# Four-tile evacuations of a split fp32 product, taken tile by tile: at the end of its last chunk and amid the next chunk's weight slabs

## The chip, the cores and the metric
One core of one Trainium2 chip runs the whole program. The metric is the device time in microseconds (us) of one execution. The engines are named PE (matmuls), DVE (vector), ACT (scalar), POOL (GpSimd) and SP (which here issues transfers).

## The reference
Two transformer-like blocks run over 512 tokens of width 1024, one after the other. Cut to what matters here:

```python
# block 1
proj = rmsnorm(h) @ w_in                               # "w1"
h = h + concat(norm(att), norm(ssm)) @ w_out           # "wo1"
q = rmsnorm(h) @ w_mem_q                               # "wmq"
k, v = rmsnorm(mem) @ w_mem_k, ... @ w_mem_v           # "wmkv"
h = h + attention(q, k, v) @ w_mem_o                   # "wmo"
h = h + peer_ffn(rmsnorm(h))                           # queries: "p1q"
# block 2
qa, ka, va, qb, kb, vb, gl = split(h2 @ w_in_2)        # "qk", "va", "vb", "gl"
gates = sigmoid(gl + b_gate)
mixed = gates[0] * (oa @ w_proj_a) + gates[1] * (ob @ w_proj_b)   # "pa", "pb"
x = x + g1 * (mixed @ w_out_2)                         # "wo2"
x = x + g2 * peer_ffn(...)                             # queries: "p2q"
```

All is fp32. `peer_ffn`, which scores 16384 experts against every token, holds most of the time; the change touches none of it but the product that makes its queries.

## The kernel before
The program is a row of phases. Each phase is one block of instruction streams, one for each engine; at its end the engines meet at a barrier, the phase's semaphores are cleared, and they meet again (`clear` in `phase_tools`, line 80; the barrier's rows carry L83). Nothing of the next phase runs before that.

`product` (line 123) is one such phase and is called thirteen times. It multiplies `srcT` (features on partitions, `kt` slabs of 128) with weights that come in `chunks` of up to 512 columns. Each fp32 factor is split in a high and a low part, and three matmuls (high by high, low by high, high by low) are added up. The streams are these:

- SP loads the weight slabs, one for each of the `kt` steps of each chunk, up to eight ahead (lines 167 to 172), then transfers that were asked for.
- ACT rounds a slab to its high part `w_hi` (line 236). It first waits until PE has done the slab `SLABS` earlier (line 234), since `w_hi` and `w_lo` are rings of `SLABS` slabs, four or two.
- DVE subtracts to get `w_lo` (line 259), which lets PE begin the slab (line 192).
- PE runs 12 matmuls in a slab: four tiles `u` (four tiles of tokens, or of output features), three matmuls each. The last of the 12 raises `multiplied` (line 202). A chunk takes four PSUM banks, and chunks alternate between two sets of four.
- When a chunk is summed up, its four tiles are evacuated from PSUM by `evacuations` (line 206), by DVE or ACT as each tile's entry says. It waits until `multiplied` has counted the whole chunk (line 210) and then takes all four tiles one behind the other, in the same instruction stream as the splits of the weights. Where an evacuation has two operations, a wait on `step` stands between them. PE waits for the evacuation of chunk c-2 before chunk c (line 185).
- The evacuation of chunk c-1 stands in the stream behind the splits of all `kt` slabs of chunk c (lines 239 and 263), or, where a norm runs as a guest in the phase (`inside`), ahead of slab `SLABS` of chunk c (`taken_at`). That of the last chunk stands at the end of the stream (lines 243 and 267).

The thirteen calls:

| phase | chunks | kt | SLABS | guest | evacuation of a tile |
|---|---|---|---|---|---|
| w1 | 4 | 8 | 4 | HeadsNorm | copy, ACT and DVE in turn |
| wo1, wmo | 2 | 8 | 4 | none | DVE adds to `h` (L2333) |
| wmq | 2 | 8 | 4 | MemoryNorm | copy, in turn |
| wmkv | 4 | 8 | 4 | two HeadsNorm | copy, in turn (two tiles) |
| p1q, p2q | 4 | 8 | 4 | TurnedBack | copy, in turn |
| va, vb | 2 | 8 | 2 | none | copy, in turn |
| gl | 4 | 8 | 2 | none | ACT, Sigmoid (L2916) |
| pa | 2 | 2 | 2 | none | DVE multiplies (L2919) |
| pb | 2 | 8 | 2 | none | DVE multiplies, then adds (L2923, L2924) |
| wo2 | 2 | 8 | 2 | none | DVE multiplies by `g1`, then adds (L2939, L2940) |

In the trace, wo1 and wo2 share the tile name `wo`. In w1 and wmkv the guest's own copies of transposed tiles (`act_end`, `dve_end`) stand ahead of the last chunk's evacuation.

Of the kernel before, what the change touches and what calls it, by code (L numbers as in the profile page):

```python
# [118 lines left out]
ON_ACT, ON_DVE = 0, 1  # L119
# [3 lines left out]
def product(nc, tag, srcT, kt, tokens, chunks, SLABS=4, transfers=(), split=None, ahead=None, halves=None, inside=()):  # L123
# [11 lines left out]
    NCH = len(chunks)  # L135
# [5 lines left out]
    with ExitStack() as ctx:  # L141
        sb, ps, sem = phase_tools(nc, ctx, tag)
# [6 lines left out]
        x_hi_ready, x_ready, w_hi_ready, w_ready, multiplied = (  # L149
            sem(n) for n in ("x_hi_ready", "x_ready", "w_hi_ready", "w_ready", "multiplied"))  # L150
# [7 lines left out]
        for guest in inside:  # L158
            guest.place(tag, sb, sem, out, chunks_out)
        taken_at = SLABS if inside else kt  # L160
# [19 lines left out]
        def _(pe):  # L180
            for c, (src, on_tokens, units) in enumerate(chunks):
# [6 lines left out]
                for k in range(kt):  # L188
# [13 lines left out]
                    last.then_inc(multiplied, 1)  # L202
# [3 lines left out]
        def evacuations(eng, which, c, steps):  # L206
            src, on_tokens, units = chunks[c]
            cols = src.shape[2] if on_tokens else tokens
            if any(e == which for e, _ in units):
                eng.wait_ge(multiplied, kt * (c + 1))  # L210
            for u, (engine, evacuate) in enumerate(units):
                if engine != which:
                    continue
                parts = evacuate(out[:, c % 2 * 4 + u, 0:cols])
                for make in parts[:-1]:
                    make().then_inc(step[which], 1)
                    steps += 1
                    eng.wait_ge(step[which], steps)
                parts[-1]().then_inc(copied[which], 1)
            return steps  # L220

        @block.scalar
        def _(act):
            steps = 0
            for c, (src, _, _) in enumerate(chunks):
                cols = src.shape[2]
                for k in range(kt):
                    s = c * kt + k
                    if c >= 1 and k == taken_at:
                        steps = evacuations(act, ON_ACT, c - 1, steps)  # L230
# [8 lines left out]
                if c >= 1 and taken_at == kt:  # L239
                    steps = evacuations(act, ON_ACT, c - 1, steps)  # L240
# [5 lines left out]
        def _(dve):  # L246
            steps = 0
            for c, (src, _, _) in enumerate(chunks):
                cols = src.shape[2]
                for k in range(kt):  # L250
                    s = c * kt + k
                    if c >= 1 and k == taken_at:
                        steps = evacuations(dve, ON_DVE, c - 1, steps)
# [9 lines left out]
                if c >= 1 and taken_at == kt:  # L263
                    steps = evacuations(dve, ON_DVE, c - 1, steps)
# [872 lines left out]
class Activations:  # L1137
# [4 lines left out]
    LOADS, SLABS, KEPT = 4, 4, 4  # L1142
# [1939 lines left out]
```

## Time and profile before

| | us |
|---|---|
| median of 3 runs | 3961.65 (3960.06 to 3962.46) |
| profiled execution | 3968.42 |
| its span on the core | 3966.6 |
| PE busy | 3626.8 (91% of the span) |
| DVE busy | 2959.2 (75%) |
| ACT busy | 1701.3 (43%) |
| POOL busy | 736.3 (19%) |

The mean granted clock of PE is 0.954 of full speed. Times in a timeline are counted from the start of the span. The duration of an operation in a row includes its end phase, so that consecutive operations on DVE or ACT start somewhat closer together than their durations say. A bracket at a row's end gives the idle time of the engine before it and what ended it. A line with "x4" merges four instructions in a row. PEclk is the granted clock of PE, where 1.00 is 2.4 GHz and 0.50 is 1.2 GHz.

### The profile page before, as it was taken

How to read it: one execution, taken by the hardware profiler on the slowest of the kernel's cores; microseconds unless marked ns; L12 is line 12 of the kernel's file. 1: busy time of each engine (PE TensorE's matmuls, PEld its weight loads, DVE VectorE, ACT ScalarE, POOL GpSimd, SP SyncE). 2: the span in 40 equal slices, each digit the busy share in tenths (PEclk: the TensorE clock that was granted, in tenths of full speed). 3: DMA queues.
4: the chain of work that ended last, by engine and by line, in shares of the span. 5: the costliest groups of instructions: out<-in, count | busy, mean ns of one | idle time of the engine just before them, and what ended most of it. 6: DMA issues, size and time to landing. Idle time of an engine off the chain costs nothing. (4 is left out here: it accounts for less than half of the span.)

```text
span 3966.6 us, 53964 instructions
## 1 busy us (share of the span) xinstructions
PE 3626.8 (91%) x19146; PEld 3149.7 (79%) x19146; DVE 2959.2 (75%) x6469; ACT 1701.3 (43%) x3187; POOL 736.3 (19%) x523
## 2 busy tenths in 40 slices
PE   7876788999999999999698898869999999999998
PEld 5545576899999988888587655657999999888887
DVE  3654463599888889999676483343999888799998
ACT  3512343233566643333344463323334666533333
POOL 0000000000333344444000000000001333345442
PEclk9978898999999999999898998989999999999999
DMA  3261222355799899999422102213456999899997
GB/s 119 87 216 43 82 91 69 110 161 168 263 307 309 301 350 402 401 400 399 163 85 80 43 1 69 69 44 116 150 161 205 319 307 308 306 401 403 403 400 285
DMA packets 371787, 853.04 MB, mean 215 GB/s; under 512 B 36016, under 2 KB 185136, under 8 KB 368944
## 3 DMA queue, kind: packets, MB, share of 16 engines
q1 hardware_dynamic: 258816, 530.45, 38.4%
q0 software_dynamic: 73728, 268.47, 17.9%
q10 hardware_dynamic: 38976, 50.68, 3.8%
q8 instruction: 154, 2.52, 0.3%
q14 instruction: 113, 0.93, 0.1%
HBM read 753.91 MB, written 94.37 MB: 214 GB/s over the span
## 5 line engine op out<-in xcount | busy, mean ns | idle before, releaser
L1091 POOL DMA_INDIRECT p2f_row<-in_expert_u_rows,p2f_index x128 | 173.6, 1356 | 1412.5 <-POOLq L83 1130.8
L1091 POOL DMA_INDIRECT p1f_row<-in_peer_u_rows,p1f_index x128 | 183.7, 1435 | 1021.0 <-POOLq L83 724.0
L1706 PE MATMUL p1v_out<-p1a_u_hi,p1v_w_hi 128*128 128x512 f32 x768 | 300.4, 391 | 4.3 <-DVE p1v_w_lo L1688 4.3
L1706 PE MATMUL p2v_out<-p2a_u_hi,p2v_w_hi 128*128 128x512 f32 x768 | 300.1, 391 | 4.3 <-DVE p2v_w_lo L1688 4.3
L1706 PE MATMUL p1v_out<-p1a_u_lo,p1v_w_hi 128*128 128x512 f32 x768 | 300.2, 391 | 0.0
L1706 PE MATMUL p1v_out<-p1a_u_hi,p1v_w_lo 128*128 128x512 f32 x768 | 300.0, 391 | 0.0
L1706 PE MATMUL p2v_out<-p2a_u_lo,p2v_w_hi 128*128 128x512 f32 x768 | 300.0, 391 | 0.0
L1706 PE MATMUL p2v_out<-p2a_u_hi,p2v_w_lo 128*128 128x512 f32 x768 | 299.8, 390 | 0.0
L1666 ACT CAST p1a_u_hi<-p1a_u 128x1024 fp32r<-128x1024 f32 x128 | 135.1, 1055 | 278.7 <-PE p1v_out L1706 277.9
L1091 POOL DMA_INDIRECT p2f_row<-in_expert_v,p2f_index x128 | 194.8, 1522 | 240.4 <-DVE p2f_sum L1114 219.0
L1666 ACT CAST p2a_u_hi<-p2a_u 128x1024 fp32r<-128x1024 f32 x128 | 135.1, 1056 | 235.1 <-PE p2v_out L1706 230.3
L1091 POOL DMA_INDIRECT p1f_row<-in_peer_v,p1f_index x128 | 179.0, 1398 | 233.5 <-DVE p1f_sum L1114 210.9
L1211 PE MATMUL p1g_pre<-p_x_hi,p1a_u_hi 128*128 128x384 f32 x576 | 198.0, 344 | 3.7 <-DVE p1a_u_lo L1201 3.7
L1211 PE MATMUL p2g_pre<-p_x_hi,p2a_u_hi 128*128 128x384 f32 x576 | 197.4, 343 | 3.7 <-DVE p2a_u_lo L1201 3.7
L1211 PE MATMUL p1g_pre<-p_x_hi,p1a_u_lo 128*128 128x384 f32 x576 | 194.5, 338 | 0.0
L1211 PE MATMUL p1g_pre<-p_x_lo,p1a_u_hi 128*128 128x384 f32 x576 | 194.2, 337 | 0.0
L1211 PE MATMUL p2g_pre<-p_x_hi,p2a_u_lo 128*128 128x384 f32 x576 | 193.7, 336 | 0.0
L1211 PE MATMUL p2g_pre<-p_x_lo,p2a_u_hi 128*128 128x384 f32 x576 | 193.6, 336 | 0.0
L1685 DVE TENSOR_TENSOR p1a_u_lo<-p1a_u,p1a_u_hi 128x1024 fp32r<-128x1024 f32 x128 | 156.4, 1222 | 25.1 <-ACT p1a_u_hi L1666 24.8
L1706 PEld LDWEIGHTS p1v_out<-p1a_u_hi,p1v_w_hi 128*128 128x128 f32 x768 | 144.9, 189 | 34.6 <-DVE p1a_u_lo L1685 4.4
L1706 PEld LDWEIGHTS p2v_out<-p2a_u_hi,p2v_w_hi 128*128 128x128 f32 x768 | 144.8, 189 | 34.4 <-DVE p2a_u_lo L1685 4.4
L1114 DVE SCALAR_TENSOR_TENSOR p2f_sum<-p2f_row,p2f_weight,p2f_sum 128x1024 f32<-128x1024 f32 x127 | 162.8, 1281 | 11.4 <-DMA p2f_row<-in_expert_v,p2f_index 9.7
(702 smaller groups left out, 10825.1 us busy)
## 6 DMA issues: line engine op xcount, KB each, us to landing
p1a_u<-in_peer_u SPq DMA_DIRECT2D x128, 512.0 KB, 4.3
p1a_u<-in_peer_v SPq DMA_DIRECT2D x128, 512.0 KB, 8.4
p2a_u<-in_expert_u SPq DMA_DIRECT2D x128, 512.0 KB, 4.4
p2a_u<-in_expert_v SPq DMA_DIRECT2D x128, 512.0 KB, 9.2
gates<-p_kept SPq DMA_DIRECT2D x20, 2048.0 KB, 12.2
acts<-p1a_a ACTq DMA_DIRECT2D x128, 192.0 KB, 4.0
p1w_a<-acts SPq DMA_DIRECT2D x128, 192.0 KB, 7.2
acts<-p2a_a ACTq DMA_DIRECT2D x128, 192.0 KB, 4.1
```

The lines of the kernel that those rows point to most:

```text
L1091: self.nc.gpsimd.indirect_dma_start(self.row[:, n % self.RING, :], None, self.u_rows if dot else self.v_rows, bass.IndirectOffsetOnAxis(ap ...
L1114: V.scalar_tensor_tensor(self.sum[:], row, weight, self.sum[:], ALU.mult, ALU.add).then_inc(self.used, 1)
L1211: last = self.nc.tensor.matmul(self.pre[:, n % 2, 0:DENSE], u[:, s, k * P:(k + 1) * P], x[:, k, P:SEQ], start=(m == 0), stop=(m == 3 * DK ...
L1666: nc.scalar.copy(v_hi[:, n % VSLABS, :], v[:, n % LOADS, :]).then_inc(v_hi_ready, 1)
L1685: V.tensor_tensor(v_lo[:, n % VSLABS, :], v[:, n % LOADS, :], v_hi[:, n % VSLABS, :], ALU.subtract).then_inc(v_ready, 1)
L1706: last = nc.tensor.matmul(out[:, o, :], lhs[:, s, t * P:(t + 1) * P], rhs[:, n % VSLABS, cols], start=(n == 0 and m == 0), stop=(n == KEYS ...
```

## The change
Three things are changed in `product`, for all callers.

1. A new semaphore `tile_done`. In the very last slab of the last chunk, PE raises it after each tile's three matmuls, and `multiplied` isn't raised for that slab. The evacuation of the last chunk waits for `tile_done` tile by tile.
2. `one_each` is true where there is no guest and `kt >= SLABS + 4`: in wo1, wmo, va, vb, gl, pb and wo2. There the evacuation of chunk c-1 is taken one tile ahead of each of the slabs `SLABS` to `SLABS + 3` of chunk c.
3. Elsewhere the place of the earlier chunks' evacuations is as it was.

```diff
--- before.py
+++ after.py
@@ -146,8 +146,8 @@
         out = ps("out", [P, 8, BANK])
         loaded = [sem(f"loaded{n}") for n in range(LOADS)]
         transferred = sem("transferred")
-        x_hi_ready, x_ready, w_hi_ready, w_ready, multiplied = (
-            sem(n) for n in ("x_hi_ready", "x_ready", "w_hi_ready", "w_ready", "multiplied"))
+        x_hi_ready, x_ready, w_hi_ready, w_ready, multiplied, tile_done = (
+            sem(n) for n in ("x_hi_ready", "x_ready", "w_hi_ready", "w_ready", "multiplied", "tile_done"))
         copied = [sem("copied_by_act"), sem("copied_by_dve")]
         step = [sem("step_act"), sem("step_dve")]
 
@@ -157,6 +157,7 @@
                 eng.wait_ge(copied[which], evacuated(upto, which))
         for guest in inside:
             guest.place(tag, sb, sem, out, chunks_out)
+        one_each = not inside and kt >= SLABS + 4
         taken_at = SLABS if inside else kt
         block = ctx.enter_context(nc.Block())
 
@@ -199,18 +200,23 @@
                                 dst, lhsT, rhs = out[:, c % 2 * 4 + u, 0:tokens], ws[:, s, tile], xs[:, k, :]
                             last = nc.tensor.matmul(dst, lhsT, rhs, start=(k == 0 and n == 0),
                                                     stop=(k == kt - 1 and n == 2), skip_group_check=True)
-                    last.then_inc(multiplied, 1)
+                        if c * kt + k == NCH * kt - 1:
+                            last.then_inc(tile_done, 1)
+                    if c * kt + k < NCH * kt - 1:
+                        last.then_inc(multiplied, 1)
                     for guest in inside:
                         guest.pe(pe, c * kt + k)
 
-        def evacuations(eng, which, c, steps):
+        def evacuations(eng, which, c, steps, chosen=None):
             src, on_tokens, units = chunks[c]
             cols = src.shape[2] if on_tokens else tokens
-            if any(e == which for e, _ in units):
+            if c < NCH - 1 and any(e == which for e, _ in units):
                 eng.wait_ge(multiplied, kt * (c + 1))
             for u, (engine, evacuate) in enumerate(units):
-                if engine != which:
+                if engine != which or chosen is not None and u not in chosen:
                     continue
+                if c == NCH - 1:
+                    eng.wait_ge(tile_done, u + 1)
                 parts = evacuate(out[:, c % 2 * 4 + u, 0:cols])
                 for make in parts[:-1]:
                     make().then_inc(step[which], 1)
@@ -226,6 +232,8 @@
                 cols = src.shape[2]
                 for k in range(kt):
                     s = c * kt + k
+                    if c >= 1 and one_each and k >= SLABS:
+                        steps = evacuations(act, ON_ACT, c - 1, steps, [k - SLABS])
                     if c >= 1 and k == taken_at:
                         steps = evacuations(act, ON_ACT, c - 1, steps)
                     if c == 0:
@@ -236,7 +244,7 @@
                     nc.scalar.copy(w_hi[:, s % SLABS, 0:cols], w[:, s % LOADS, 0:cols]).then_inc(w_hi_ready, 1)
                     for guest in inside:
                         guest.act(act, s)
-                if c >= 1 and taken_at == kt:
+                if c >= 1 and taken_at == kt and not one_each:
                     steps = evacuations(act, ON_ACT, c - 1, steps)
             for guest in inside:
                 guest.act_end(act, NCH * kt)
@@ -249,6 +257,8 @@
                 cols = src.shape[2]
                 for k in range(kt):
                     s = c * kt + k
+                    if c >= 1 and one_each and k >= SLABS:
+                        steps = evacuations(dve, ON_DVE, c - 1, steps, [k - SLABS])
                     if c >= 1 and k == taken_at:
                         steps = evacuations(dve, ON_DVE, c - 1, steps)
                     if c == 0:
@@ -260,7 +270,7 @@
                                             w_hi[:, s % SLABS, 0:cols], ALU.subtract).then_inc(w_ready, 1)
                     for guest in inside:
                         guest.dve(dve, s)
-                if c >= 1 and taken_at == kt:
+                if c >= 1 and taken_at == kt and not one_each:
                     steps = evacuations(dve, ON_DVE, c - 1, steps)
             for guest in inside:
                 guest.dve_end(dve, NCH * kt)
```

## Rows read from the trace of the kernel before

**Rows 1.** The page, part 1: busy us (share) xinstructions of each engine.
```profile
PE 3626.8 (91%) x19146; PEld 3149.7 (79%) x19146; DVE 2959.2 (75%) x6469; ACT 1701.3 (43%) x3187; POOL 736.3 (19%) x523
```

**Rows 2.** Timeline, end of wo1: start us, us, engine line op [idle <-releaser].
```profile
403.93 0.39 PE L200 MATMUL wo_out<-wo_w_lo,wo_x_hi 128*128 128x512 f32 x1
...
405.97 0.39 PE L200 MATMUL wo_out<-wo_w_lo,wo_x_hi 128*128 128x512 f32 x1
406.40 2.48 DVE L2333 TENSOR_TENSOR main_h<-main_h,wo_out 128x512 f32<-128x512 f32 x4 [7.14 <-PE wo_out L200]
409.85 1.06 ACT L977 ACTIVATE n_xn<-main_h 128x1024 f32<-128x1024 f32 x1 [13.70 <-PEq L83]
```

**Rows 3.** Timeline at the end of wmq, ACT and DVE.
```profile
481.91 1.29 DVE L278 COPY mb_q<-wmq_out 128x512 f32<-128x512 f32 x2 [9.53 <-PE wmq_out L200]
...
484.06 0.40 ACT L232 CAST wmkv_x_hi<-mb_memT 128x256 fp32r<-128x256 f32 x1 [1.08 <-PEq L83]
```

**Rows 4.** Timeline of ACT in gl, around its first evacuation.
```profile
2468.50 0.62 ACT L236 CAST gl_w_hi<-gl_w 128x512 fp32r<-128x512 f32 x1 [2.10 <-PE gl_out L200]
2469.14 1.28 ACT L2916 ACT_TABLE_LOAD   x1
2470.44 2.42 ACT L2916 ACTIVATE b_mixT<-gl_out,cols 128x512 f32<-128x512 f32 x4
2472.74 0.63 ACT L236 CAST gl_w_hi<-gl_w 128x512 fp32r<-128x512 f32 x1
...
2477.28 0.62 ACT L236 CAST gl_w_hi<-gl_w 128x512 fp32r<-128x512 f32 x1 [2.71 <-PE gl_out L200]
```

**Rows 5.** Timeline of ACT at the end of gl and the start of pa.
```profile
2518.08 2.42 ACT L2916 ACTIVATE b_qkT<-gl_out,cols 128x512 f32<-128x512 f32 x4 [2.50 <-PE gl_out L200]
2521.45 0.62 ACT L232 CAST pa_x_hi<-b_oaT 128x512 fp32r<-128x512 f32 x1 [0.95 <-PEq L83]
```

**Rows 6.** Timeline of DVE in pa, both chunks' evacuations.
```profile
2534.00 2.47 DVE L2919 TENSOR_TENSOR b_mixT<-b_mixT,pa_out 128x512 f32<-128x512 f32 x4
2538.18 2.48 DVE L2919 TENSOR_TENSOR b_mixT<-b_mixT,pa_out 128x512 f32<-128x512 f32 x4 [1.70 <-PE pa_out L200]
```

**Rows 7.** Timeline of PE and DVE at the end of pb.
```profile
2588.14 0.69 DVE L259 TENSOR_TENSOR pb_w_lo<-pb_w,pb_w_hi 128x512 fp32r<-128x512 f32 x1 [2.03 <-ACT pb_w_hi L236]
...
2588.75 0.68 DVE L2923 TENSOR_TENSOR b_qkT<-b_qkT,pb_out 128x512 f32<-128x512 f32 x1
...
2589.46 0.69 DVE L2924 TENSOR_TENSOR b_mixT<-b_mixT,b_qkT 128x512 f32<-128x512 f32 x1
...
2590.07 0.68 DVE L2923 TENSOR_TENSOR b_qkT<-b_qkT,pb_out 128x512 f32<-128x512 f32 x1
...
2592.50 0.39 PE L200 MATMUL pb_out<-pb_x_hi,pb_w_lo 128*128 128x512 f32 x1
...
2598.73 0.69 DVE L2924 TENSOR_TENSOR b_mixT<-b_mixT,b_qkT 128x512 f32<-128x512 f32 x1
```

**Rows 8.** Timeline of DVE at the end of wo2.
```profile
2657.17 0.69 DVE L2940 TENSOR_TENSOR main_h<-main_h,wo_out 128x512 f32<-128x512 f32 x1
```

**Rows 9.** Timeline of DVE at the end of w1.
```profile
129.71 1.28 DVE L286 COPY b_u<-w_out 128x512 f32<-128x512 f32 x2
```

**Rows 10.** Transfers of 2160:2200, in va: issues, KB each, us to landing.
```profile
b2v_masks<-in_masks SPq DMA_DIRECT2D x1, 1536.0 KB, 8.0
```

**Rows 11.** Windows after two starts of PE: PE busy (xcount), PEclk, DMA share, GB/s.
```profile
488.70:492.70 4.00, 3.95 (x9) 0.50 0.98 345
2525.60:2529.60 4.00, 3.92 (x12) 0.64 0.12 41
```

**Rows 12.** Timeline of PE, first matmul after an idle stretch, in p1g and p1v.
```profile
1011.79 0.44 PE L1211 MATMUL p1g_pre<-p_x_hi,p1a_u_hi 128*128 128x384 f32 x1 [3.65 <-DVE p1a_u_lo L1201]
...
1409.55 0.77 PE L1706 MATMUL p1v_out<-p1a_u_hi,p1v_w_hi 128*128 128x512 f32 x1 [4.29 <-DVE p1v_w_lo L1688]
```

**Rows 13.** Waits of PE in 2510:2540, before pa: us in total, times, longest.
```profile
PE pa_out L200 <- DVE pa_w_lo L259: 7.6, 1, 7.6
```

## The prediction

> **What bounds the kernel now.** I read the page first: PE is busy 91% of the span [rows 1], nearly all of it in the expert phases, which the change doesn't touch. So the question is not which engine bounds the whole, but what ends each of the thirteen `product` phases, since each is closed off by a barrier. For that I read the timeline at the end of each. The reader is to see there that PE's last matmul isn't the end: a row of evacuations follows it, the barrier begins when the last of them is done, and nothing else is late. In wo1 the last matmul ends at 405.97 + 0.39 = 406.36, the four additions run from 406.40 for 2.48 us, to 408.88, and the next phase's first operation starts at 409.85, 0.97 later [rows 2]. In gl the last sigmoid ends at 2518.08 + 2.42 = 2520.50 and the next phase starts 0.95 later [rows 5]; in wmq it is 483.20 and 0.86 [rows 3]. The distance from the last evacuation to the next phase is nearly constant, so what shortens the evacuation shortens the program, one to one. I then read the timelines inside the phases, for the places that the moved evacuations leave and enter.
>
> **What the signal of each tile gives.** The last slab's tiles don't finish together. In wo1 the third matmul of the first tile starts at 403.93 and that of the fourth at 405.97 [rows 2]: 2.04 us for three tiles, 0.68 each. Four additions take 2.48 us of which the last is 0.68, so they start 0.60 apart. An evacuation that follows tile by tile therefore keeps up with PE, and only the fourth is left behind the last matmul.
>
> - wo1: the fourth addition starts at 406.40 as before and ends at 407.08 instead of 408.88: 1.80. wmo ends in the same pattern. Together 3.60.
> - wmq, p1q, p2q, va, vb: each engine has two copies, and DVE's pair, 1.29 us, is the later [rows 3]; the same pair stands at the other four ends. The fourth tile's copy alone takes 0.69, so 0.60 each, 3.00 together. va's 1536 KB of masks land 8.0 us after their issue [rows 10], which the trace has at 2171, some 25 us before va's end; they don't take the end's place.
> - gl: four sigmoids 2.42, one 0.69 (the second to fourth start 0.58 apart, so ACT keeps up too): 1.73 [rows 5].
> - pa: the first chunk's additions start at 2534.00, so DVE is free for another at 2536.40. Tile 4 is there at 2538.14 by [rows 6], the others 0.68, 1.36 and 2.04 earlier. The four then start at 2536.40, 2537.00, 2537.60 and 2538.20, and end at 2538.88 instead of 2538.18 + 2.48 = 2540.66. That is 1.78 at best; I take 1.70.
> - w1 and wmkv: nothing. The phase's own two copies on DVE start at 129.71 with no wait of their own before them [rows 9]: they queue behind the guest's last copy, when all tiles are long done. wmkv has the same order.
>
> **What taking one tile for each slab gives.** In pb a tile costs DVE two operations, 1.32 us from one tile to the next (2588.75 to 2590.07). The first chunk's four therefore keep DVE until 2588.75 + 4 x 1.32 = 2594.03, over a us beyond the last matmul's end, 2592.50 + 0.39 = 2592.89. The end is 2598.73 + 0.69 = 2599.42 [rows 7]. After the change the first chunk's are out of the way; the last chunk's start when its first tile is done, 2592.93 - 2.04 = 2590.89, and DVE is then the slower: three tiles of 1.32 and a last one of 0.71 + 0.69 (start to start of the pair, and the second's duration) give 2596.25. The gain is 3.17. wo2 has the same pattern at 1.33 a tile and ends at 2657.17 + 0.69 = 2657.86 [rows 8], with its last matmul as far ahead. I take 3.15 each, 6.30 together.
>
> In gl, ACT's first evacuation includes a table load of 1.28 and comes in one piece of 0.64 + 1.30 + 2.42 us ahead of the next slab's cast. Slabs are 2.10 + 0.62 = 2.72 apart. From the cast at 2468.50 to the one at 2477.28, three slabs later, it is 8.78 instead of 8.16 [rows 4]: 0.62 is lost, at the third chunk's start. One tile at a time, load and sigmoid end 0.64 + 1.30 + 0.69 = 2.63 after the cast, within the 2.72. The loss goes: 0.62. In wo1, wmo, va and vb the earlier chunk's evacuation is hidden under PE's slabs before and after, and moving it gives nothing.
>
> **What it costs.** The moved evacuations stand ahead of a weight split in DVE's or ACT's stream, in front of work that PE needs; that is what they could cost. In pb the split of a slab starts 2.72 after the one before and DVE is free 0.61 later (2588.14, 2588.75); a tile's pair takes 1.41, to 2590.16, and the next split would be due at 2590.86 [rows 7]. So 0.70 is spare on DVE, and PE has about 1.2 more, since it begins a slab that long after its `w_lo` is there. For the single operations, 0.60 to 0.69, the spare time is larger. On ACT the new place adds no wait: the cast behind it waits for a later count of `multiplied` than the evacuation does. Nothing is queued behind the waits on `tile_done` but the evacuations themselves, since all splits are over. No transfer is moved on SP's queue and nothing on POOL's. The added semaphore lengthens the clearing at most: between the last evacuation and the next phase lie 0.97 us in wo1, with 18 semaphores [rows 2], and 0.86 in wmq, with 27 by the code [rows 3]. So it isn't the count that sets it; I take zero, with 0.01 each, 0.13 in all, as the bound above.
>
> **PE's clock.** Each phase starts after an idle stretch with the granted clock at 0.50, 1.2 GHz. In wmkv it stays there over the whole 4 us, in pa it averages 0.64 [rows 11]: 9 matmuls against 12 in 4 us. A slow matmul starts 0.43 after the last, a fast one 0.23; 12 in 4.0 us are 6 slow ones (6 x 0.43 + 6 x 0.23), and that is the fewest at any product's start behind wo1 but va's. The most is 14, counted by their durations, and wmkv has 12. The phases' starts shift by a few us, so this is drawn anew. Going the full way at one start is 8 x 0.2 = 1.6 us; over a dozen starts with both signs I allow 3 either way. The Trainium skill, page "TensorE: Matmul & The Clock Gate", Part 1, says the same kernel shows different counts of cold matmuls according to when its first one falls; by that rule too the sum stays and only its spread grows. No start should change its kind: an idle of 3.65 us left the clock up (0.44 for 384 columns) and one of 4.29 let it fall (0.77) [rows 12], while the idle before pa, now 7.6 [rows 13], is shortened by no more than gl's 1.73, to 5.9, and is the shortest of those that lose more than 0.60.
>
> **The sum.** 3.60 + 3.00 + 1.73 + 1.70 + 6.30 + 0.62 = 16.95 us. On the profiled execution, 3968.42 becomes 3951.5. It stands 6.8 above the median, and I take the same gain off the median: 3961.65 - 16.95 = 3944.7.
>
> **The rivals.**
> - The ends are set by something that the timelines don't show, or the per-tile signal comes late because PE raises it only when its queue drains. Then the tails stay and only gl's 0.62 is gained: 3961.0. Against it: the 0.9 us or so behind the last evacuation in three phases with different last engines, and casts of weights, which wait on the same kind of signal amid PE's matmuls and start every 2.72 us. Chance 0.05.
> - PE's clock falls out badly: wmo (7 slow matmuls now), pa (6) and the 12s all go to 14. That is 0.2 x (7 + 8 + 6 x 2) = 5.4 us: 3950.1. Nothing speaks for it but the spread in [rows 11]. Chance 0.06.
> - ACT reloads its table at each change between sigmoid and cast, now that they alternate in gl. A slab would cost ACT 0.52 + 0.58 + 2 x 1.28 = 3.66, 0.94 over the 2.72, in 12 slabs 11.3 us: 3956.0, which is within 0.2%. Against it: the casts behind the four sigmoids have no load before them [rows 4]. The Trainium skill, page "ScalarE: Activation LUTs", section "Rules for kernel authors", says to group calls by table set and finish one before switching, which speaks against this edit; it prices a switch at 2.66 us, by which it would be 0.52 + 0.58 + 5.32 - 2.72 = 3.70 a slab and the time an estimated 3989. The same page has copies in every set, and there the trace agrees. Chance 0.03.
> - Slower: the evacuations, now in front of the weight splits, come to stand on PE's path. With rings of two slabs, whatever delays a split beyond its slack delays PE. If each were fully exposed it would cost 8 x 0.60 in wo1 and wmo, 8 x 0.60 in va and vb, 12 x 0.58 in gl and 8 x 1.32 in pb and wo2: 27.1 us, so 3971.8. It decides where a tile's operations pass 1.41 + 0.70 + 1.2 = 3.3 us for each slab in pb; they are at less than half of that [rows 7]. Chance 0.03.
>
> **How the numbers follow.** The forecast, 3944.7, has 0.83; its own range is 3941 to 3949 by the clock's 3 us either way and about 1 for the run to run spread of the median. For 8 in 10 it would do nearly alone; with the clock's rival taken in it is 3940.5 to 3950.5. A measurement can tell about 0.2%, 7.9 us, from no change: faster means below 3953.7. Faster gets 0.83 + 0.06 = 0.89 (less 0.01 for what I have not thought of: 0.88), within 0.2% gets 0.05 + 0.03 and that 0.01, 0.09, and slower 0.03.
>
> **What would show it.** In the profile after, wo1's additions stand apart, 0.68 from start to start, the last ending 0.7 after PE; pb's and wo2's last eight start some 2 us before PE's last matmul ends; gl has its sigmoids singly between casts, one table load, casts every 2.72 us throughout; pb's `w_lo` still start 2.72 apart. If the gaps of PE inside gl, pb or wo2 grow, the slower rival is at work. If the phases' ends move up and the total doesn't, the time went to the starts: PEclk in the first 4 us of each phase shows it.

## The result and the profile after

The changed kernel takes 3939.67 us (median of 5 runs, 3932.46 to 3945.17) against 3962.46 for the kernel before beside it (3960.06 to 3964.1): a ratio of 0.9944, 95% interval 0.9929 to 0.9958. The profiled execution took 3938.45, its span is 3936.6, the mean granted clock 0.957. The forecast was 3944.7 in a range of 3940.5 to 3950.5, so the direction and most of the size were right, and the time lies 0.8 us below the range. Timed on three further occasions, on three chips, it came to 3946.23, 3938.90 and 3939.61; one of the four times lies in the range. Over all 21 of its executions the mean is 3940.4 (standard deviation 5.3), over 96 of the kernel before 3962.9 (3.9). The gain is thus 22.5 us, and the standard error from these two spreads is 1.2, so some 20 to 25. The sum of the prediction was 16.95. Some 5 us are to be explained beyond it. One execution of all those reported below, of tile_only, took 4992.31 us at a granted clock of 0.692; it counts in no ratio, and without it that kernel's median is 3947.71 instead of 3947.96.

The page of the changed kernel, part 1, which answers to [rows 1]:

```profile
PE 3615.3 (92%) x19146; PEld 3144.1 (80%) x19146; DVE 2961.4 (75%) x6469; ACT 1699.8 (43%) x3187; POOL 745.2 (19%) x523
```

The same instructions run, and DVE and ACT are busy for the same time. PE is busy for 11.5 us less, with the same 19146 matmuls. A shorter tail can't do that: it takes idle time away. It is a first sign that matmuls ran at another clock, though from one pair of profiles.

The ends of the phases look as forecast. The timeline of the changed kernel at the end of wo1 (start us, us, engine, line, op, [idle before it <- releaser]), which answers to [rows 2]:

```profile
398.81 2.72 DVE L2343 TENSOR_TENSOR main_h<-main_h,wo_out 128x512 f32<-128x512 f32 x4 [7.49 <-PE wo_out L201]
...
400.42 0.39 PE L201 MATMUL wo_out<-wo_w_lo,wo_x_hi 128*128 128x512 f32 x1
402.50 1.06 ACT L987 ACTIVATE n_xn<-main_h 128x1024 f32<-128x1024 f32 x1 [11.91 <-PEq L83]
```

The four additions now begin 2.00 us ahead of PE's last end (400.81) and are through 0.72 behind it; the barrier still takes 0.97. The four additions last 2.72 instead of 2.48 us, because they follow PE's tiles, 0.68 apart. ACT in gl, around the first evacuation, answers to [rows 4], and its end to [rows 5]:

```profile
2432.73 0.62 ACT L244 CAST gl_w_hi<-gl_w 128x512 fp32r<-128x512 f32 x1 [2.10 <-PE gl_out L201]
2433.37 1.28 ACT L2926 ACT_TABLE_LOAD   x1
2434.67 0.69 ACT L2926 ACTIVATE b_mixT<-gl_out,cols 128x512 f32<-128x512 f32 x1
2435.45 0.62 ACT L244 CAST gl_w_hi<-gl_w 128x512 fp32r<-128x512 f32 x1
2435.98 0.68 ACT L2926 ACTIVATE b_mixT<-gl_out,cols 128x512 f32<-128x512 f32 x1
2438.17 0.62 ACT L244 CAST gl_w_hi<-gl_w 128x512 fp32r<-128x512 f32 x1 [1.51 <-PE gl_out L201]
...
2495.97 2.73 ACT L2926 ACTIVATE b_qkT<-gl_out,cols 128x512 f32<-128x512 f32 x4 [2.73 <-PE gl_out L201]
2499.66 0.62 ACT L240 CAST pa_x_hi<-b_oaT 128x512 fp32r<-128x512 f32 x1 [0.96 <-PEq L83]
```

The casts stay 2.72 apart (2432.73, 2435.45, 2438.17), also over the table load, which is the only one in gl; sigmoids stand singly between them. DVE in pb, one slab of the last chunk and then the end, answers to [rows 7]:

```profile
2549.08 0.69 DVE L269 TENSOR_TENSOR pb_w_lo<-pb_w,pb_w_hi 128x512 fp32r<-128x512 f32 x1 [2.03 <-ACT pb_w_hi L244]
2549.69 0.68 DVE L2933 TENSOR_TENSOR b_qkT<-b_qkT,pb_out 128x512 f32<-128x512 f32 x1
2550.40 0.69 DVE L2934 TENSOR_TENSOR b_mixT<-b_mixT,b_qkT 128x512 f32<-128x512 f32 x1
2551.80 0.69 DVE L269 TENSOR_TENSOR pb_w_lo<-pb_w,pb_w_hi 128x512 fp32r<-128x512 f32 x1 [0.70 <-ACT pb_w_hi L244]
...
2568.14 0.69 DVE L2933 TENSOR_TENSOR b_qkT<-b_qkT,pb_out 128x512 f32<-128x512 f32 x1 [1.98 <-PE pb_out L201]
...
2572.84 0.69 DVE L2934 TENSOR_TENSOR b_mixT<-b_mixT,b_qkT 128x512 f32<-128x512 f32 x1
```

The splits are 2.72 apart, with the 0.70 us of DVE's spare time that the prediction worked out in the bracket of the last of them. PE's last matmul of pb ends at 2570.15; DVE is through at 2573.53.

**All thirteen tails.** The tail is here the time from the end of a product's last matmul to the end of the barrier behind it; the next phase's first operation starts some 0.07 us later. In us, before and after: wo1 3.41, 1.62; wmo 3.40, 1.63; wmq 2.12, 1.53; p1q 2.22, 1.63; p2q 2.22, 1.64; va 2.21, 1.63; vb 2.21, 1.63; gl 3.34, 1.61; pa 3.40, 1.62; pb 7.42, 4.28; wo2 7.92, 4.75; w1 2.77, 2.78; wmkv 1.97, 1.97. The differences sum up to 16.3; with the 0.62 inside gl it is 16.9, against the 16.95 that was forecast. So the 5 us lie outside the products' ends.

### The profile page after: what moved, and what is told of

Its sections match the earlier page's. It is cut to its first block and busy times, and to the rows that moved or that the text cites. A ratio compares the mean times of both kernels' runs of the same rounds, so it can differ in the third digit from the quotient of the medians.

```text
span 3936.6 us, 53976 instructions
## 1 busy us (share of the span) xinstructions
PE 3615.3 (92%) x19146; PEld 3144.1 (80%) x19146; DVE 2961.4 (75%) x6469; ACT 1699.8 (43%) x3187; POOL 745.2 (19%) x523
## 5 line engine op out<-in xcount | busy, mean ns | idle before, releaser
L1101 POOL DMA_INDIRECT p2f_row<-in_expert_u_rows,p2f_index x128 | 189.3, 1479 | 1401.7 <-POOLq L83 1115.5
L1101 POOL DMA_INDIRECT p2f_row<-in_expert_v,p2f_index x128 | 182.6, 1427 | 233.8 <-DVE p2f_sum L1124 209.6
L1695 DVE TENSOR_TENSOR p2a_u_lo<-p2a_u,p2a_u_hi 128x1024 fp32r<-128x1024 f32 x128 | 156.5, 1222 | 23.4 <-ACT p2a_u_hi L1676 18.9
```

What stands on the lines that cost most here:

```text
L1101: self.nc.gpsimd.indirect_dma_start(self.row[:, n % self.RING, :], None, self.u_rows if dot else self.v_rows, bass.IndirectOffsetOnAxis(ap ...
L1695: V.tensor_tensor(v_lo[:, n % VSLABS, :], v[:, n % LOADS, :], v_hi[:, n % VSLABS, :], ALU.subtract).then_inc(v_ready, 1)
```

## The experiments

Each kernel ran in a comparison of five rounds with the kernel before on the same chip. The ratio and its 95% interval are of that comparison, and a gain in us is worked out from the ratio. The expectations call their rivals theory A and theory B anew in each run. First, what scatters by itself.

**before_again**: the kernel before, unchanged.

> The kernel before, once more, as a control. Theory A (the change is worth the 16.95 us of the sum, and the rest of the measured 22 us is the part of each PE start that runs at the low clock, which is drawn anew in every execution): between two profiled executions of this same kernel, single phases differ by 1 to 8 us where PE is slow for longer, and the whole by 2 to 8 us; the ratio to itself is 1.000 within 0.1%. Theory B (the change is worth 22 us, the missing 5 being a saving in some phase that I overlooked): the phases agree within 1 us between the two executions, and so does the whole within about 2 us.

3962.51 us, ratio 1.0 (0.9991 to 1.0009), span 3969.7. This set the scale for what follows: a median of such a run can be told from another to about 0.1%, 4 us. One pair of profiles can't: ahead of wo1, in code that is the same in all kernels, the modulation phase alone took 108.8 and 109.1 us in the two profiles of the kernel before, and 101.5, 109.3 and 106.0 in profiles of the changed one. So phases are compared one by one, over many profiles, and only a difference that comes back in each is read.

**after_again**, **after_third** and **after_fourth**: the changed kernel, unchanged.

> The changed kernel, once more. Theory A: the timed gain is 17 us with a scatter of some us from one set of executions to the next, so anything from 14 to 22 here; the tails behind the last matmul of the twelve affected products are as short as in the first profile to 0.1 us, while the phases that gained outside of them (the modulation phase, dif, the tile norm, p1c, p1g) come out otherwise than in the first profile. Theory B: 22 to 23 us again, with the same phases shorter as in the first profile.

3946.23 us, 0.9957 (0.9944 to 0.9970). The tails are the same as in the first profile, and the modulation phase fell back from 101.5 to 109.3 us, as theory A had it; but p1c, among the phases that theory A expected to come out otherwise, took 259.7 us again.

> The changed kernel a third time, for its mean and its phases. Theory A (locked): wmq 56.8, mat 35.6, wmo 52.0, p1q 95.9 and p1c 259.7 us once more, each within 0.3; these phases with the two norms give some 3 us over the tails' sum, and the gain is about 19 us, 16 to 22 in one set. Theory B (drawn anew): single ones of them fall back to the length of before (less the tail), and the gain is 17 on the mean.

3938.90 us, 0.9936 (0.9919 to 0.9952). The five phases that theory A names took 56.8, 35.6, 51.9, 95.8 and 259.7 us, each as it said.

> The changed kernel a fourth time, beside the run with the turned order and for the mean of its gain. Theory A (locked): 3 us over the tails' 17, so 20 on the mean of all sets, 16 to 24 in this one; wmq 56.8, mat 35.6, p1q 95.9 and p1c 259.7 us in its profile. Theory B: 17 on the mean and other lengths.

3939.61 us, 0.9943 (0.9930 to 0.9956), with 56.7, 35.6, 95.8 and 259.7 us for the four phases. Three of the four ratios of the changed kernel lie under the one that 16.95 us would give, 0.9957, and the fourth is at it.

**tile_only**: the signals of each tile alone.

> Only the signal of each tile in the last chunk; the earlier chunks are evacuated where they were. From the rows of before: wo1 and wmo 3.60, wmq, p1q, p2q, va and vb 3.00, gl 1.73, pa 1.78, together 10.1 us. In pb and wo2 nothing, since DVE is still at the first chunk's eight operations until 2594.03 when the last tile is done (2592.9), and can begin no earlier than before. Theory A: 10 us on the mean, 7 to 14 in one set. Theory B: the missed 5 us come with the shorter tails, so about 14.

```diff
-        one_each = not inside and kt >= SLABS + 4
+        one_each = False
```

3947.96 us, 0.9965 (0.9952 to 0.9978): 14 us gained, between 9 and 19, where the tails give 3.6 + 3.0 + 1.73 + 1.78 = 10.1. The end of pb on DVE:

```profile
2573.35 0.39 PE L201 MATMUL pb_out<-pb_x_hi,pb_w_lo 128*128 128x512 f32 x1
...
2579.57 0.69 DVE L2934 TENSOR_TENSOR b_mixT<-b_mixT,b_qkT 128x512 f32<-128x512 f32 x1
```

6.52 us from PE's end to DVE's, the same as 2592.89 to 2599.42 in [rows 7]: the signals alone give pb nothing, for DVE still has the first chunk in front of it.

**each_only**: the other half alone; the last chunk waits for `multiplied` as before.

> Only the earlier chunks taken one tile for each slab; the last chunk waits for the whole as before. From the rows of before: pb starts its last evacuation at 2592.93 instead of 2594.04 (1.11), wo2 as much (1.15), gl loses no 0.62 at its third chunk: together 2.9 us. The two halves give 13.0 alone and 16.95 together, as pb and wo2 gain their 2.0 each from the early tiles only when the first chunk is out of the way. Theory A: 3 us, 0 to 6 in one set. Theory B: 8 us if the missed gain lies within the products' slabs, 3 if it lies at the tails.

```diff
-                        if c * kt + k == NCH * kt - 1:
-                            last.then_inc(tile_done, 1)
-                    if c * kt + k < NCH * kt - 1:
-                        last.then_inc(multiplied, 1)
+                    last.then_inc(multiplied, 1)
...
-            if c < NCH - 1 and any(e == which for e, _ in units):
+            if any(e == which for e, _ in units):
...
-                if c == NCH - 1:
-                    eng.wait_ge(tile_done, u + 1)
```

3959.20 us, 0.9993 (0.9984 to 1.0001). Its tails are 6.32 in pb and 6.79 in wo2, 1.10 and 1.13 shorter, and gl loses its stall: 2.85 by the sum, 2.8 measured, between 0 and 6. The two halves of the change give 1.1 and 0 in pb, and 3.14 together, since each removes what the other would leave last. The times show no 5 us with this half, and some 4 beyond the tails in tile_only, within wide intervals.

**wo1_tail**: of the whole change, only wo1's last chunk follows tile by tile.

> Only wo1's last chunk is evacuated tile by tile: everything behind wo1 starts 1.80 us earlier. In the profiles so far, phases between wmq and p1c have the same length in all three executions with the old starts and another, equally constant one in all three with the changed starts. Theory A (locked): the clock's rises and falls lie on a grid of their own, phases fall on it in a fixed way behind the modulation phase, and the shift moves them on it. Then, as in the changed kernel: the norm behind wo1 0.8 us longer, wmq 1.2 shorter and mat 1.0 shorter at an unchanged wmq tail, so that more than the 1.80 is gained by the end of mat: 3.2. Theory B (drawn anew): the phases behind wo1 differ from before at random, some up, some down, and do not repeat those of the run with the delay; on the mean 1.8 us.

```diff
-        one_each = not inside and kt >= SLABS + 4
+        one_each = False
+        by_tile = tag == "wo1"
...
-                        if c * kt + k == NCH * kt - 1:
+                        if by_tile and c * kt + k == NCH * kt - 1:
...
-                    if c * kt + k < NCH * kt - 1:
+                    if not by_tile or c * kt + k < NCH * kt - 1:
...
-                if c == NCH - 1:
+                if by_tile and c == NCH - 1:
```

3958.51 us, 0.9990 (0.9981 to 0.9998): 4.0 us, between 0.8 and 7.5, from a tail that is 1.79 shorter.

**wo1_delay**: the kernel before, with 1.6 us of dead work on DVE behind wo1's last evacuation.

> The kernel before with dead work at the end of wo1: two additions of 512 columns and one of 352 on scratch, 1.6 us. Nothing else. [...] Theory A (locked): the phases from the norm behind wo1 to p1c have the lengths of the run with wo1's tail alone, each within 0.2 us; with the norm 0.8 longer, wmq 1.2 and mat 1.0 shorter the delay is nearly given back by the end of mat (+0.2), and the whole is at most about 1 us slower than before, or faster. Theory B (drawn anew): 1.6 us slower on the mean, with phases unlike those of the other run.

```diff
+            if tag == "wo1":
+                for n, cols in enumerate((BANK, BANK, DEAD)):
+                    nc.vector.tensor_tensor(w[:, n, 0:cols], w[:, 3 + n, 0:cols], w[:, 3 + n, 0:cols], ALU.add)
```

3961.18 us, 0.9991 (0.9982 to 1.0000). The delay is there, wo1's tail is 5.04 instead of 3.41, and the program is not slower for it. Three windows of each of three profiles tell what happened behind wo1: the norm, wmq, and the memory attention `mat`, in this order (us, busy time of each engine with the count of its instructions, then PEclk, DMA share and GB/s). before_again:

```profile
409.85:425.50 15.65, 5.82 (x32) 5.58 (x32) 6.57 (x13) 7.22 (x13) 0.00 (x0) 0.59 0.00 0
425.50:484.10 58.60, 48.51 (x208) 39.69 (x208) 21.91 (x39) 19.49 (x37) 0.00 (x0) 0.91 0.26 90
545.00:581.50 36.50, 34.06 (x224) 30.29 (x224) 21.01 (x72) 16.16 (x49) 0.00 (x0) 0.95 0.01 1
```

wo1_tail:

```profile
402.50:418.80 16.30, 6.52 (x32) 6.28 (x32) 6.57 (x13) 7.22 (x13) 0.00 (x0) 0.58 0.00 0
418.90:476.20 57.30, 47.21 (x208) 38.82 (x208) 21.83 (x39) 19.39 (x37) 0.00 (x0) 0.91 0.27 92
537.00:572.50 35.50, 32.58 (x224) 29.24 (x224) 21.02 (x72) 16.17 (x49) 0.00 (x0) 1.00 0.01 1
```

wo1_delay:

```profile
407.10:423.40 16.30, 6.53 (x32) 6.29 (x32) 6.57 (x13) 7.22 (x13) 0.00 (x0) 0.57 0.00 0
423.50:480.70 57.20, 47.24 (x208) 38.81 (x208) 21.82 (x39) 19.38 (x37) 0.00 (x0) 0.91 0.27 93
541.60:577.10 35.50, 32.58 (x224) 29.24 (x224) 21.02 (x72) 16.17 (x49) 0.00 (x0) 1.00 0.01 1
```

In all three the counts are 32, 208 and 224 matmuls. Only PE's busy time differs: 5.82 against 6.5 in the norm, 48.5 against 47.2 in wmq, and 34.1 against 32.6 in `mat`, where PEclk is 0.95 or 1.00. The two edited kernels, one with a tail of 1.62, the other of 5.04, agree with each other to 0.03 us and differ from the kernel before alike. From barrier to barrier the three phases changed by +0.75, -1.3 and -1.0, so nearly all of the 1.63 us of the delay came back.

**wo1_delay2**: 3.43 us of dead work, by three more operations.

> As the run with dead work at wo1's end, but 3.4 us of it instead of 1.6 (five additions of 512 columns and one of 352). Theory A (locked): the phases have the old lengths again, the norm behind wo1 15.7, wmq 58.6, mat 36.6, p1q 97.6 and p1c 261.3 us, and the delay is paid in full: 3.4 us slower than before, and some 5 slower than with the shorter delay, which gave about 1.9 us back by the end of wmo. Theory B (drawn anew at each start): these phases differ from both at random.

```diff
-                for n, cols in enumerate((BANK, BANK, DEAD)):
+                for n, cols in enumerate((BANK, BANK, BANK, BANK, BANK, DEAD)):
```

3962.35 us, 1.0004 (0.9995 to 1.0012): 1.6 us lost, between -2 and 4.8. Norm, wmq and `mat` took 15.5, 58.5 and 36.7 us from first operation to first operation, the lengths of the kernel before (15.6, 58.6 and 36.6), as theory A said. So there are sets of lengths, and a delay changes from one to the other and back. Which set comes isn't fixed by wo1's tail alone, as the next kernels show.

**pool_add**: the changed kernel, with the second operation of pb's and wo2's evacuation on POOL, each behind DVE's first.

> The changed kernel with the second operation of a tile in pb and wo2 (the addition, on SBUF alone) moved to POOL, which is idle there; DVE keeps the multiplication. Behind PE's last matmul stand now 3.4 us in pb and 3.8 in wo2 before the barrier, since DVE needs 1.32 a tile. With one operation DVE keeps pace with PE (0.68 a tile), and 0.7 on DVE and one addition on POOL are left. A row for such an addition doesn't exist in the trace; between 0.7 (as on DVE) and 2.0 us. At 1.0 the two tails shorten by about 1.6 and 2.0 us, 3.6 together; at 2.0 POOL doesn't keep pace and little is left. Both theories say the same for the tails, and for the whole 3.6 with a scatter of some us by the clock.

```diff
+        if pooled:
+            @block.gpsimd
+            def _(pool):
+                for n, add in enumerate(pooled):
+                    pool.wait_ge(copied[ON_DVE], n + 1)
+                    add(pool).then_inc(added, 1)
...
-            lambda: nc.vector.tensor_tensor(mixT[:, f, :], mixT[:, f, :], sig[:, f, :], ALU.add)]
+    def add(f):
+        return lambda pool: pool.tensor_tensor(mixT[:, f, :], mixT[:, f, :], sig[:, f, :], ALU.add)
```

In wo2 the product by `g1` goes to a buffer in SBUF instead of back into PSUM, and in both products DVE takes a tile's place again only when POOL is done with it. 3938.76 us, 0.9940 (0.9927 to 0.9953), as the changed kernel. The end of pb, DVE and POOL:

```profile
2572.53 2.73 DVE L2942 TENSOR_TENSOR b_qkT<-b_qkT,pb_out 128x512 f32<-128x512 f32 x4 [1.98 <-PE pb_out L202]
...
2573.30 4.96 POOL L2945 TENSOR_TENSOR b_mixT<-b_mixT,b_qkT 128x512 f32<-128x512 f32 x4 [9.01 <-DVE b_qkT L2942]
```

Four additions take POOL 4.96 us, 1.28 each by their mean, against 0.69 on DVE. POOL then is the slower of the two, and at this price nothing is left of the 1.6 and 2.0 us that an addition of 1.0 us would have given. It is through 3.72 us behind PE's last end (2574.54), where DVE alone is through after 3.38 (2570.15 to 2573.53); pb's tail is 4.96 instead of 4.28. Half of the 0.68 more is thus between POOL's end and the barrier's: the next phase starts 1.31 us behind the last evacuation instead of 0.97. wo2's tail is 4.66 and 4.75, the same to 0.1. The Trainium skill, page "GPSIMD Engine Reference", section "Elementwise — side-by-side cycle accounting", gives an addition of two fp32 inputs of 2048 elements as 1.96 times as long there as on DVE; here, at 512, it is 1.86 times.

**last_two**: the changed kernel, with PE's order in the last two slabs of pb and wo2 turned round, so that tiles finish further apart.

> The changed kernel, with PE's order in the last two slabs of pb and wo2 turned: tiles 1 and 2 of the last slab but one, then the same two of the last, then tiles 3 and 4 in both. Tiles 1 to 4 are then done 3.40, 2.72, 1.36 and 0 us before the last matmul's end instead of 2.04, 1.36, 0.68 and 0. DVE, at 1.32 a tile, starts 3.4 ahead and the fourth tile 0.6 behind the end, so the tails shrink from 4.28 to 2.9 in pb and from 4.75 to 3.4 in wo2: 2.7 us together if PE doesn't wait for the last slab's split, which is there about 1.4 us after the slab before begins, as the first two tiles take 1.36. Both theories say the same for the tails; for the whole 2.7 less than the changed kernel, with the clock's scatter.

```diff
+                if early:
+                    for k, u in ((kt - 2, 0), (kt - 2, 1), (kt - 1, 0), (kt - 1, 1), (kt - 2, 2), (kt - 1, 2), (kt - 2, 3),
+                                 (kt - 1, 3)):
...
+                        if k == kt - 1:
+                            last.then_inc(tile_done, 1)
```

3938.74 us, 0.9938 (0.9926 to 0.9951). The end of pb:

```profile
2571.65 0.69 DVE L2948 TENSOR_TENSOR b_qkT<-b_qkT,pb_out 128x512 f32<-128x512 f32 x1 [1.06 <-PE pb_out L220]
...
2574.66 0.39 PE L220 MATMUL pb_out<-pb_x_hi,pb_w_lo 128*128 128x512 f32 x1
...
2576.34 0.69 DVE L2949 TENSOR_TENSOR b_mixT<-b_mixT,b_qkT 128x512 f32<-128x512 f32 x1
```

DVE starts 3.40 us ahead of PE's end instead of 2.01, and the tails are 2.89 and 3.36, 2.8 us less together. The kernel with the shortest tails is 0.9 us ahead of the changed kernel on the same chip, which the intervals can tell neither from nothing nor from the 2.8.

pool_add and last_two both run the changed kernel's instructions up to pb, and yet `mat` took 36.7 us in both, the length of the kernel before, where all four profiles of the changed kernel have 35.6. p1q took 97.8 and 96.9 in them instead of 95.8. So the lengths aren't settled by the code, and that they are locked, as theory A had it since wo1_tail, isn't so in general. One phase behaved otherwise. Over the 13 profiles up to here, p1c and p2c (the first phases of the expert layers, behind p1q and p2q) last 261.3 us in each kernel whose query product keeps its tail of 2.22, and 259.7 in each where it is 1.63, whatever the phases ahead did. The difference is in their first instructions. before_again and the changed kernel, PE at the start of p1c:

```profile
749.25 5.44 PE L1311 MATMUL p1c_score<-p1f_row,p1m_qT 128*128 128x128 f32 x32 [2.31 <-PEq L83]
```

```profile
737.18 3.81 PE L1321 MATMUL p1c_score<-p1f_row,p1m_qT 128*128 128x128 f32 x32 [1.73 <-PEq L83]
```

32 score matmuls, 1.63 us faster, behind an idle time that is 0.58 shorter. Their windows in before_again show the clock:

```profile
749.20:751.20 2.00, 1.95 (x14) 1.98 (x14) 0.00 (x0) 1.98 (x3) 0.00 (x0) 0.78 0.00 0
751.20:753.20 2.00, 2.00 (x11) 2.00 (x11) 0.00 (x0) 1.98 (x4) 0.00 (x0) 0.50 0.00 0
```

and in the changed kernel:

```profile
737.10:741.10 4.00, 3.81 (x32) 3.65 (x32) 0.08 (x1) 3.93 (x5) 0.00 (x0) 1.00 0.00 0
```

PE resumes at 2.4 GHz in both. In the first it falls to 1.2 GHz about a us later, while the scores run; in the second it doesn't. What tells whether the shorter idle did that, or the place to which the phase was shifted, are three last kernels.

**queries_tail**: the kernel before, with the signals of each tile in p1q and p2q alone.

> Only p1q and p2q take the signal of each tile; all other products are as in the kernel before. The two tails shrink from 2.22 to 1.63 us, 1.2 together, and PE's idle time ahead of the 32 score matmuls at the start of p1c and p2c goes from 2.31 to 1.73. Theory A (the shorter idle keeps PE's clock up): both groups of 32 score matmuls take 3.81 instead of 5.44 us, p1c and p2c last 259.7 instead of 261.3, and the whole gains 1.2 + 2 x 1.63 = 4.4 us, a ratio of 0.9989, although nothing ahead of p1q is changed. Theory B (it is where p1c comes to lie that counts, shifted by all the tails ahead of it): the queries come 0.6 us earlier than in the kernel before, not 18, so at least one of the two groups stays at 5.44, and the gain is 1.2 to 2.8.

```diff
-        by_tile = tag == "wo1"
+        by_tile = tag in ("p1q", "p2q")
```

(against wo1_tail.) 3957.71 us, 0.9988 (0.9977 to 0.9998): 4.8 us, between 0.8 and 9.1. The tails alone give 1.2, theory B up to 2.8 and theory A 4.4, so the time can't choose between them; the starts of p1c and p2c do:

```profile
740.78 3.81 PE L1322 MATMUL p1c_score<-p1f_row,p1m_qT 128*128 128x128 f32 x32 [1.73 <-PEq L83]
...
2761.74 3.81 PE L1322 MATMUL p2c_score<-p2f_row,p2m_qT 128*128 128x128 f32 x32 [1.73 <-PEq L83]
```

**queries_back**: the changed kernel, with p1q and p2q as they were.

> The changed kernel, with p1q and p2q back at one wait for the whole last chunk. Their tails are 2.22 again, the idle 2.31. Theory A: both groups of 32 score matmuls take 5.44 again, p1c and p2c 261.3, and against the changed kernel 4.4 us are lost: some 18 of its 22.5 us of gain are left, a ratio near 0.9954. Theory B: the shift ahead of p1c is as in the changed kernel but for 0.6, so p1c stays at 259.7 and only 1.2 to 2.8 us are lost.

```diff
+        by_tile = tag not in ("p1q", "p2q")
...
-                if c == NCH - 1:
+                if by_tile and c == NCH - 1:
```

3947.05 us, 0.9961 (0.9948 to 0.9974):

```profile
742.47 5.37 PE L1322 MATMUL p1c_score<-p1f_row,p1m_qT 128*128 128x128 f32 x32 [2.33 <-PEq L83]
...
2751.87 5.44 PE L1322 MATMUL p2c_score<-p2f_row,p2m_qT 128*128 128x128 f32 x32 [2.33 <-PEq L83]
```

**queries_delay**: the changed kernel, signals and all, and one dead addition of 0.60 us behind the last evacuation of p1q and p2q.

> The changed kernel, signals of each tile kept in p1q and p2q, with one dead addition of 128x512 on DVE behind their last evacuations, 0.60 us: the barrier starts that much later and PE's idle is 2.33 again. Theory A (the idle alone counts, not the signals): as with p1q and p2q put back, scores 5.44, p1c and p2c 261.3, some 4.4 us lost for 1.2 us of dead work. A rival C (the signals themselves change PE's state): scores stay at 3.81 and 1.2 us are lost.

```diff
+            if tag in ("p1q", "p2q"):
+                nc.vector.tensor_tensor(w[:, 0, 0:BANK], w[:, 4, 0:BANK], w[:, 4, 0:BANK], ALU.add)
```

3946.65 us, 0.9961 (0.9948 to 0.9974):

```profile
745.68 5.32 PE L1323 MATMUL p1c_score<-p1f_row,p1m_qT 128*128 128x128 f32 x32 [2.31 <-PEq L83]
...
2759.31 5.43 PE L1323 MATMUL p2c_score<-p2f_row,p2m_qT 128*128 128x128 f32 x32 [2.31 <-PEq L83]
```

All six starts went as theory A says, and theories B and C fall: neither the shift ahead of p1c matters nor the kind of signal. Two dead additions, 1.2 us of work, cost some 6 us against the changed kernel by the two ratios (0.9961 against the mean of its four, 0.9945), with half-widths of some 5 and 3 us; 4.4 was expected. Here too the starts show the cause and the times only fit it. Taken over all 16 profiles, 16 starts behind an idle of 2.31 to 2.33 took 5.32 to 5.44 us, and 16 behind 1.73 took 3.81. p1c and p2c are 1.6 us shorter each from barrier to barrier in the latter.

In each of these 32 starts PE had been at 2.4 GHz until the idle. In the 16 behind the longer idle the clock fell between 0.25 us ahead of the first matmul and 1.3 us behind it.

queries_back and queries_delay also gave another set of lengths for norm, wmq and `mat`: 14.9, 57.6 and 36.6 us, with wo1 as in the changed kernel. Why these phases come out so isn't shown.

## Why the prediction was right and where it was wrong

**The tails**: right, term by term. wo1 1.79 for 1.80, wmo 1.77 for 1.80; the five pairs of copies 0.58 to 0.59 for 0.60; gl 1.73 for 1.73; pa 1.78 for 1.70; pb 3.14 for 3.17 and wo2 3.17 for 3.15; w1 and wmkv nothing. tile_only and each_only show that pb's 3.14 needs both halves of the change.

**The stall in gl**: right. From its first matmul to its last, PE took 89.76 instead of 90.38 us, and the wait of 0.3 us for `w_lo` in it is gone.

**What it costs**: nothing, as worked out, by the 0.70 us left on DVE ahead of pb's splits and casts that stay 2.72 apart in gl.

**PE's clock, the step that failed.** The prediction gave a shorter idle no effect on the clock behind it, and so put this term at 0 with a margin of 3. It had two halves, and the first was wrong in its reading: "No start should change its kind: an idle of 3.65 us left the clock up (0.44 for 384 columns)" [rows 12]. That row shows the first matmul only. The windows of the kernel before go on:

```profile
1011.70:1013.70 2.00, 1.91 (x9) 1.91 (x10) 1.97 (x5) 0.00 (x0) 1.69 (x2) 0.81 0.41 102
1013.70:1015.70 2.00, 2.00 (x8) 2.00 (x7) 1.97 (x2) 0.00 (x0) 1.39 (x3) 0.50 1.01 391
```

The clock did fall, 1.2 us behind the first matmul. In all 32 starts of p1g and p2g over the 16 profiles it fell, from 1.3 us ahead of the first matmul to 1.5 behind it. So an idle that seemed harmless wasn't. Nor does each phase start at 0.50, as the prediction has it: at p1c and p2c PE resumes at 1.00, the idles of 2.31 ahead of them weren't priced, and the clock fell 1 us into the scores. The change takes 0.59 from both and the fall goes: 2 x 1.63 = 3.26 us. The Trainium skill, page "TensorE: Matmul & The Clock Gate", Part 1, section "What's actually happening", says that the point at which the clock goes up varies from run to run with where the first matmul lands. Of the clock's fall the traces show the like at `mat`: the same idle of 2.06 to 2.08 us was followed by a fall in nine profiles and by none in seven. At p1c and p2c it doesn't go so: the outcome was the same in all 16 starts of each kind.

The second half, "this is drawn anew" and "over a dozen starts with both signs I allow 3 either way", was right in kind. In the phases norm, wmq and `mat` behind wo1, kernels with the changed kernel's ends show three outcomes: together, wmq's tail set aside, they are 1.3 to 1.6, 1.0 to 1.2 and 0.2 to 0.5 us shorter than in before_again. The start of p1g went the other way, behind the same idle of 3.65. In the changed kernel:

```profile
998.20:1000.20 2.00, 2.00 (x6) 2.00 (x7) 1.97 (x4) 0.00 (x0) 1.70 (x2) 0.50 0.54 100
1000.20:1003.20 3.00, 3.00 (x11) 3.00 (x11) 2.96 (x6) 0.00 (x0) 2.32 (x3) 0.50 0.99 348
```

There, as in its three repeats and in tile_only, the clock fell 1.1 to 1.3 us ahead of the first matmul and was back 5.5 to 5.8 behind it, where in the kernel before it was low from 1.2 to 4.6. Some 2.1 us more of matmuls ran at half speed, an estimated 1.1 us lost.

tile_only's 13.9, between 9 and 19, fits 10.1 and 3.26. With the 3.26 the sum of the whole change becomes 16.95 + 3.26 = 20.2. The measured 22.5 has an interval of 20 to 25, so what is left, 2.3, is about two standard errors. Its cause stays open. The median of 3961.65 less 20.2 is 3941.4, 1.8 above what was measured and inside the range; that the time fell 0.8 below the range is the 3.26 and this rest together.

**The rivals.** That the ends are set by something else fell with the tails; that ACT reloads its table fell with the one load in gl; that the evacuations stand on PE's path fell with the spacing of the splits. That the clock falls out badly had the right place and the wrong sign.

**What stays open.** That wo1_delay's 1.6 us came back is seen in the three phases behind it, but not why these fall into the set that they do; a kernel that holds wo1's end and moves only the norm wasn't tried. Between idles of 1.73 and 2.31 us nothing was measured at p1c. last_two is not told from the changed kernel in the whole. The 3.26 us are shown by the matmuls of p1c and p2c; the times of the whole program fit them but are too wide to prove them.

## What to carry to other kernels

Before pricing a shorter idle at its own length, look at what PE does in the microseconds behind it, by the granted clock in short windows and not by the first matmul's duration. Here 0.59 us off an idle was worth 2.2. Where an evacuation has two operations and each chunk's is queued behind the next chunk's splits, signals for each tile and an earlier place pay off together: 3.14 us in pb, against 0 and 1.1 alone. And a kernel whose phases scatter by 8 us from run to run should be compared phase by phase over several profiles: one pair of them shows 30 us where 22 are gained.

## What the runs showed of the hardware

- A dead operation of 0.60 us on DVE in front of a barrier made 32 later matmuls 1.5 to 1.6 us slower, since PE's idle time went from 1.73 to 2.31 and the clock then fell to 1.2 GHz while they ran. Over all 16 such starts the fall came between 0.25 us ahead of the first of them and 1.3 us behind it, and in 10 of them the first matmul took 0.35 us, as at 2.4 GHz.
- 1.63 us of dead work at another barrier cost nothing (0.9991, 0.9982 to 1.0000); in the three phases behind it, some 1.5 us came back by PE's clock. 3.43 us cost 1.6, with an interval that takes in both 0 and 3.4.
- A signal raised by PE amid its stream lets DVE begin within 0.04 us of that matmul's end, and raising four in a slab costs PE nothing: its matmuls there stay 0.23 apart.
- An addition of 128x512 in fp32 takes POOL 1.28 us and DVE 0.69. DVE did a dependent pair in 1.32 a tile by itself, and the second operation on POOL made the two tails 4.96 and 4.66 instead of 4.28 and 4.75.
